# Six turns of the modulation sums by transposes, and the dt projection over column quarters

## What is computed

```python
ada = silu(c) @ w_ada + b_ada          # 9 sequences x 6 sets of 1024
sh_m, sc_m, gt_m, sh_f, sc_f, gt_f = split(ada, 6)
h = rmsnorm(x, g_mix) * (1 + sc_m) + sh_m
u, v, z, xbc, dt_raw = split(h @ w_in)  # dt_raw: 8 columns, one per head
dt = softplus(dt_raw + dt_bias)
...                                     # gMLP heads, convolution and SSD heads
x = x + gt_m * mix
h = rmsnorm(x, g_ffn) * (1 + sc_f) + sh_f
x = x + gt_f * moe(h)                   # top 4 of 32 experts, each 3 matrices of 1024 x 1024
```

## Time and profile before

| | |
|---|---|
| median of 3 runs | 1198.17 us (1196.61 to 1198.84) |
| span of the profiled execution | 1193.2 us |
| what lies around the span, against the median | 5.0 us |
| PE, DVE, ACT, POOL busy in it | 1144.8, 293.9, 153.4, 32.1 us |
| mean granted TensorE clock | 0.985 of full speed |

### The profile page before, as it was taken

How to read it: one execution, slowest core, us unless ns; L and a number is a source line. 1 busy time by engine, 2 the same in 40 slices (tenths; PEclk the granted TensorE clock), 3 DMA queues, 4 the chain that set the end, 5 groups by cost and what they waited for, 6 DMA issues and landing times.

```text
span 1193.2 us, 15523 instructions
## 1 busy us (share of the span) xinstructions
PE 1144.8 (96%) x6471; PEld 532.9 (45%) x6472; DVE 293.9 (25%) x667; ACT 153.4 (13%) x258; POOL 32.1 (3%) x46
## 2 busy tenths in 40 slices
PE   5999999999999999999999999999999999999995
PEld 2666556554353524243535353434343444434332
DVE  3254422422121213030303031212121212121143
ACT  1442141311000000000101010101010101011002
POOL 1030201000000000000000000000000000000000
PEclk9899999999999999999999999999999999999998
DMA  9574567649999999999999999999999999999992
GB/s 381 226 272 156 221 272 313 263 183 429 417 428 422 428 422 427 426 427 427 425 428 428 427 426 429 429 430 426 429 429 430 427 428 429 430 427 420 429 419 90
DMA packets 38788, 452.67 MB, mean 379 GB/s; under 512 B 4176, under 2 KB 6608, under 8 KB 7632
## 3 DMA queue, kind: packets, MB, share of 16 engines
q1 hardware_dynamic: 37984, 449.31, 89.8%
q0 software_dynamic: 752, 2.60, 0.6%
HBM read 447.99 MB, written 3.91 MB: 379 GB/s over the span
## 4 chain that ended last, share of the span: by engine, by line
PE 76%; DMA 19%; ACT 2%; DVE 1%; issue 1%; SPq 0%; DVEq 0%
PE ps L620 75%; DMA arena<-in_w_exp 18%; ACT arena L1320 1%; DMA arena<-in_w_front 1%; DVE arena L1404 1%; DMA arena<-in_xT 1%; PE ps L1007 0%; SPq L517 0%; PE ps L776 0%; DVE arena L1810 0%; DVE arena L1808 0%; DVE arena L1789 0%; ACT arena L1180 0%; PE ps L797 0%; PE ps L1065 0%
## 5 line engine op out<-in xcount | busy, mean ns | idle before, releaser
L620 PE MATMUL ps<-arena 128*64 128x512 f32 (+10 forms) x6226 | 1115.5, 519 | 37.5 <-DMA arena<-in_w_exp 14.3
L620 PEld LDWEIGHTS ps<-arena 128*64 128x64 f32 (+4 forms) x6226 | 505.4, 147 | 638.4 <-issue 568.4
L1320 ACT ACTIVATE arena<-ps 128x1024 f32<-128x1024 f32 x45 | 44.4, 1021 | 516.4 <-PE ps L620 516.4
L1746 DVE TENSOR_SCALAR arena<-ps 128x1024 f32<-128x1024 f32 x15 | 18.3, 1223 | 266.0 <-PE ps L620 266.0
L1404 DVE TENSOR_TENSOR arena<-arena 128x1024 f32<-128x1024 f32 (+11 forms) x91 | 66.2, 749 | 53.1 <-ACT arena L1328 16.8
L1404 DVE TENSOR_TENSOR arena<-arena,ps 128x320 f32<-128x320 f32 (+2 forms) x116 | 57.0, 494 | 69.2 <-PE ps L620 64.2
L1754 DVE TENSOR_SCALAR arena<-ps 128x1024 f32<-128x1024 f32 x15 | 18.4, 1224 | 183.6 <-PE ps L620 183.6
L1328 ACT ACTIVATE arena<-arena 128x1024 f32<-128x1024 f32 x16 | 16.9, 1057 | 243.8 <-DVE arena L1746 228.3
L1739 DVE COPY arena<-arena 128x64 f32 (+3 forms) x32 | 5.0, 193 | 124.9 <-PE ps L620 124.9
L1404 DVE TENSOR_TENSOR arena<-ps,arena 128x64 f32<-128x64 f32 (+10 forms) x39 | 13.2, 354 | 40.1 <-PE ps L620 35.3
L1732 DVE TENSOR_SCALAR arena<-arena 128x64 f32<-128x64 f32 (+3 forms) x96 | 23.0, 302 | 0.1
(11 more groups left out here) (147 smaller groups left out, 176.2 us busy)
## 6 DMA issues: line engine op xcount, KB each, us to landing
arena<-in_w_exp SPq DMA_DIRECT2D x180, 2048.0 KB, 22.0
arena<-in_w_front SPq DMA_DIRECT2D x38, 1024.0 KB, 9.3
arena<-in_w_exp SPq DMA_DIRECT2D x24, 1024.0 KB, 24.0
arena<-in_s0T SPq DMA_DIRECT2D x1, 2048.0 KB, 15.9
out_ssmsT<-arena POOLq DMA_DIRECT2D x4, 512.0 KB, 5.3
arena<-in_xT SPq DMA_DIRECT2D x1, 1280.0 KB, 6.1
out_yT<-arena SPq DMA_DIRECT2D x4, 320.0 KB, 3.3
arena<-in_vec SPq DMA_DIRECT2D x1, 898.0 KB, 18.7
```

What stands on the lines that cost most here:

```text
L620: return pe.matmul(o, l, r, start=start, stop=stop, skip_group_check=True)
L1320: A(moe[name].rearrange("p (a b) -> p a b", a=2), ps[:, bank:bank + 2, :], ACT.Copy).then_inc(done, 1)
L1746: V.tensor_scalar(halves("g"), blocks(0), LIMIT, None, ALU.min).then_inc(g_ready, 1)
```

## The change

Each `ada_turn` becomes four transposes of 128 x 128, one for each chunk of the bank's 512 columns. The two `kk` sums come out apart, and DVE adds them: two additions of bias for the two halves (reading `kk` 0), a wait for its own step, and two additions of `kk` 1. `gather9` leaves the constants, and `ident` moves into their first load, which grows from 73 KB to 128 KB; the second load shrinks.

The dt projection has `w_dt` stationary, 32 columns wide (8 of k, the rest are neighbours that nobody reads), and all 320 columns of `hT` move. The eight products go to four quarters of PSUM bank 3, k and k + 4 adding up in one. ACT copies the bank to a new view `dtT`; behind `ada_sums(GT_M)` PE waits for that copy and runs three matmuls with `gather32`, which add the quarters and turn the result.

A wait of DVE on the ranks uses the ordinary step counter in place of a semaphore of its own.

```diff
             def ada_turn(n, s, bank):
                 pe.wait_ge(adat_ready, n + 1)
-                for m in range(KC):
-                    c = (m % 4) * P
-                    last = mm(ps[:, bank, m * 9:m * 9 + 9], adat[:, n % 2, c:c + P],
-                              cn("gather9")[:, (m // 4) * 9:(m // 4) * 9 + 9])
+                for c in range(0, AW, P):
+                    last = pe.transpose(ps[:, bank, c:c + P], adat[:, n % 2, c:c + P], cn("ident"))
                 last.then_inc(ada_tr, 1)
...
             pe.wait_ge(xbc_line, 1)
-            for t, (t0, n) in enumerate(TILES):
-                for k in range(KC):
-                    last = mm(ps[0:n, 3, t * H:(t + 1) * H], hT[:, k, t0:t0 + n], w_dt[:, k, :], k == 0, k == KC - 1)
-                    if t == 0 and k == 0:
-                        last.then_inc(front_used, 1)
-            last.then_inc(dt_mm, 1)
+            for k in range(KC):
+                g = 32 * (k % 4)
+                last = mm(ps[g:g + 32, 3, 0:T], w_dt[:, k * H:k * H + 32], hT[:, k, :], k < 4, k >= 4)
+                if k == 0:
+                    last.then_inc(front_used, 1)
+            last.then_inc(dtT_mm, 1)
             pe.wait_ge(xbc_line, 5)
             ada_sums(GT_M, 7)
             pe.wait_ge(ld_vec2, 16)
             pe.wait_ge(ld_con, 16)
+            pe.wait_ge(dtT_ready, 1)
+            for t, (t0, n) in enumerate(TILES):
+                last = mm(ps[0:n, 3, 320 + t * H:320 + (t + 1) * H], dtT[:, t0:t0 + n], cn("gather32")[:, 0:H])
+            last.then_inc(dt_mm, 1)
             pe.wait_ge(xbc_line, KC)
... ACT, ahead of the last conv_out
+            act.wait_ge(dtT_mm, 1)
+            A(dtT, ps[:, 3, 0:T], ACT.Copy).then_inc(dtT_ready, 1)
             conv_out(KC - 1)
... DVE, ada_rows
-                tt(ada[:, s], ps[:, bank, 0:KC * 9].rearrange("p (m b) -> p m b", m=KC), wide(bada[:, s, :], 2, 9),
-                   ALU.add).then_inc(ada_ready, 1)
+                turned_sums = ps[:, bank, :].rearrange("p (c k h b) -> p k h c b", c=4, k=2, h=2)[:, :, :, :, 0:9]
+                for h in range(2):
+                    part = ada[:, s, 4 * h:4 * h + 4]
+                    ins = tt(part, turned_sums[:, 0, h], wide(bada[:, s, 4 * h:4 * h + 4], 2, 9), ALU.add)
+                step(ins)
+                for h in range(2):
+                    part = ada[:, s, 4 * h:4 * h + 4]
+                    ins = tt(part, part, turned_sums[:, 1, h], ALU.add)
+                ins.then_inc(ada_ready, 1)
```

More of the change, by code:

```diff
@@ L117 @@
 ROW, ROWW = layout([("g_v", AW), ("dt_bias", H), ("a_log", H), ("d_skip", H), ("b_router", NE)])
-CON, CONW = layout([("ones", P), ("gather9", 2 * (1 + NSEQ)), ("upto", P), ("after", P), ("ident", P), ("before", P),
+CON, CONW = layout([("ones", P), ("ident", P), ("upto", P), ("after", P), ("before", P),
                     ("upto_s", TS), ("after_s", TS), ("seq", NSEQ), ("rep", TS), ("iota", WIDE), ("thr", PASSES), ("eidx", P),
@@ L159, in constants @@
     which = np.arange(P)
-    for half in range(2):
-        for s in range(1 + NSEQ):
-            out[(which % 32 == s) & (which // 32 % 2 == half), CON["gather9"][0] + half * (1 + NSEQ) + s] = 1.0
     put("gather32", (which[:, None] % NE == np.arange(NE)[None, :]).astype(np.float32))
@@ L272, in build @@
         vsq = cat[:, :, 0:AW]
+        dtT = view(acc_at + 2 * H * P, [T])
         def tiny(shape):
@@ L407, in build @@
         w_router = vc("w_router", KC)
-        w_dt = vc("w_dt", KC)
+        w_dt = vec[:, VEC["w_dt"][0]:VEC["w_dt"][0] + (KC - 1) * H + 32]
         w_sp = vc("w_sp", AH)
@@ L435, in build @@
             sem(n) for n in ("line_ready", "xbc_mm", "xbc_line", "conv_begun", "conv_done", "xbc_ready"))
+        dtT_mm, dtT_ready = sem("dtT_mm"), sem("dtT_ready")
         dt_mm, dt_abs, dt_exp, dt_one, dt_ln, dta_ready = (
@@ L1468, in _ @@
             dve.wait_ge(ld_row, 16)
-            step(tt(dtx[:, 0:2, :], ps[:, 3, 0:2 * H].rearrange("p (t h) -> p t h", t=2), wide(rw("dt_bias"), 1, 2), ALU.add))
-            step(tt(dtx[0:TS, 2, :], ps[0:TS, 3, 2 * H:3 * H], rw("dt_bias", TS), ALU.add))
+            step(tt(dtx[:, 0:2, :], ps[:, 3, 320:320 + 2 * H].rearrange("p (t h) -> p t h", t=2), wide(rw("dt_bias"), 1, 2), ALU.add))
+            step(tt(dtx[0:TS, 2, :], ps[0:TS, 3, 320 + 2 * H:320 + 3 * H], rw("dt_bias", TS), ALU.add))
             step(V.tensor_scalar(dtr, dtx, 0.0, None, ALU.max))
@@ L1701, in _ @@
                                              picked[0:rows, a:b, :], ALU.add, ALU.mult)
-            ins.then_inc(rank_read, 1)
-            dve.wait_ge(rank_read, 1)
+            step(ins)
             step(V.tensor_scalar(rank[:, 0:NE, 0:2], rank[:, 0:NE, 0:2], -1.0, None, ALU.add))
```

4 lines of the change are left out of this document (2 added, 2 removed).

## The result

The changed kernel takes 1187.6 us in the median of 5 runs (1185.97 to 1192.68), the kernel before, on the same chip, 1198.28 us (1196.61 to 1199.32): ratio 0.9932, 95% interval 0.9915 to 0.9948. I had predicted 1194.1 us and a range down to 1191.3, so the direction was right and the gain, 10.7 us by these medians, 2.6 times the 4.1 that I had forecast. A part of that is luck. A single run of the changed kernel has a standard deviation of 2.6 us, so the mean of 11 is good to about 0.8 us (an estimate from that scatter).

What follows compares the result with a forecast made beforehand. Bound: PE finishing its first expert unit, then a stream of fixed length. Terms -0.7 - 0.15 - 3.75 + 0.5 = -4.1 against span 1193.2 give 1189.1, plus 5.0 around it 1194.1 us; range 1191.3 to 1197.0.

Steps and rivals of the forecast that it cites:

- the 5.0 around it: Time outside the profiled span: 5.0 us added to put the sum on the median of the runs.
- The clock, the term that failed: v's first tile: PE, sparse from 73.3 to 82.9, probably meets a low clock; +0.5 us, between 0 and 1.7.
- Turn 1 (-0.7): Ahead of the xbc projection: -1.25 on PE, +0.4 on DVE, constants landing 0.14 later; together -0.7 us.
- dt and turn 2 (-0.15): Up to v's first tile: 4.1 us saved, 1.4 left at v's start, -0.15 after waiting for v's second unit.
- turn 1's shift: Turn 1's gain of 0.7 us, applied throughout to later times, which were given on the clock of before.
- the three waits that I named: Ahead of v: PE waits for ada2's last unit (about 2 us), ACT (about 2 us), and `rep_read` until 82.9.
- Turns 3, 4, 5 (-1.25 each): Turns with PE work on both sides and no transfer due: -1.25 us each, -3.75 together.
- my outer bound of -4.1: Largest gain allowed for turns 3 to 5 together, with four transposes at 0.107 us each.
- the first rival: More arrives: v's second unit does not hold PE, the whole 1.4 comes, 1192.7 us, in the extreme 1190.1; chance 0.13.
- a rival with two more low stretches: The clock falls more often in turns and sparse stretches: one more gives 1195.8 us, two 1197.5; chance 0.16.
- The stream of fixed length: After PE finishes its first expert unit, the rest takes a fixed time, so front microseconds gained count at the end.

Runs made afterwards that it cites:

- e1: The kernel before, measured again with no edit: 1197.11 us, ratio 0.9999.
- e6: The kernel before with two dense matmuls of 256 columns added ahead of turn 5, which stays as gathering matmuls: 1195.8 us, ratio 0.9982.
- e10: The kernel before with turn 5 alone done by four transposes and DVE's four additions: 1196.31 us, ratio 0.999.
- e12: The kernel before with the 2 MB of state issued behind v's second unit, not ahead of it: 1196.5 us, ratio 0.9991.
- e13: The kernel before with turn 5's eight gathering matmuls moving 64 columns each in place of 9: 1196.31 us, ratio 0.9988.
- e14: The kernel before with turn 5 by transposes, each of the four done four times: 1196.11 us, ratio 0.9987.
- e3: The kernel before with only the new dt projection, turns still by gathering matmuls: 1197.38 us, ratio 1.0002.
- e11: The kernel before with the new dt projection, and the 2 MB of state issued behind v's second unit: 1197.84 us, ratio 0.9987.
- e2: The kernel before with all six turns by transposes, dt as before: 1192.13 us, ratio 0.9954.
- e4: The changed kernel, measured again with no edit: 1191.57 us, ratio 0.9947 against the kernel before.
- e8: The changed kernel with 28 unneeded transposes of 128 x 128 as filling in PE's waits around turn 1: 1189.52 us, ratio 0.9922.
- e5: The changed kernel with the 2 MB of state issued behind v's second unit, not ahead of it: 1190.0 us, ratio 0.9933.
- e7: The changed kernel with seven unneeded matmuls of 256 columns in PE's waits around turn 1: 1187.87 us, ratio 0.9912.
- e9: The changed kernel with the state issued late, seven filler matmuls around turn 1 and two ahead of turn 5: 1186.4 us, ratio 0.9904.

## Why the prediction was wrong

**The baseline, 3 us.** I put the profiled span of before and "the 5.0 around it" on the median. What lies around the span is 2.0 us. The other 3 were that the profiled execution was quicker than the median, mainly in the clock: its B is 44.2, while the six other kernels with the old dt and the old turn 2 (e1, e6, e10, e12, e13, e14) have 45.9 to 47.4. A sum made against its rows then counts the low stretches of a lucky execution. This is no further term beside the next one: it is why the rows around v had so little to save.

**The clock, the term that failed: +0.5 predicted.** Behind turn 5 the six profiles with gathers of 9 columns (before, e1, e3, e6, e11, e12) each have a low stretch, and E is 46.3 to 46.4. None of the eight with four transposes has it, nor have e13 and e14. The term was -1.6 there, shown by e13 and e14 at the old length of the turn. So the step that failed is the clock's sign: I let the change cost clock around v and nothing elsewhere, and it gave clock back behind turn 5. I had looked for the clock only where the change made PE sparse, and had not read the windows behind the turns for stretches that it could take away. Around v, where I had placed the +0.5, B is 43.9 and 45.9 in the two profiles of the changed kernel against 46.7 in the mean of the seven with the old front: about -1.8 in place of my -0.15 and +0.5. That is less firm than turn 5: the profile of the changed kernel against that of before alone gives -0.3, B scatters by 3 us within the seven, and no experiment separates the clock in it from the rest. Turns 1 to 4 have no such effect that repeats: C and D are the same to 0.01 us within each form.

**Turn 1 (-0.7).** The xbc projection started at 32.09 in place of 32.51, so -0.4 in the two first profiles; in the others the start moves between 31.8 and 34.0 with the low clock that lies over it, and A of the changed kernel (65.7, 65.9) is 0.6 to 0.8 under the shown before and 1.15 under the mean of the seven kernels with the old front (67.0). Right within about its bounds, -0.3 to -1.1. DVE's four additions took 0.61 where I had 0.65.

**dt and turn 2 (-0.15).** The mechanism was right in each step in the changed kernel's profile: v began at 81.94 (82.9 by my sum less turn 1's shift, 82.2), behind the three waits that I named, and PE then waited for v's second unit, which landed at 86.60, 0.85 earlier than before, where I had turn 1's 0.7. That dt gives nothing by itself was measured (e3, e11). But there the reason is not the landing: in e3 PE never waits for the unit, and in e11 the unit is there early; in both profiles the saving goes to the low clock in v's first tile. The landing holds PE where turn 2 is done by transposes (e2, the changed kernel, e4, e8). Whether the whole kernel keeps what e5 gave back is open.

**Turns 3, 4, 5 (-1.25 each).** 1.35, 1.40 and, by e14 less the four-transpose kernels without a wait, 44.7 - 43.4 = 1.3. Mis-sized by about a tenth of a microsecond each: a turn at full clock takes 0.44 and not the 0.48 that I took, and before, turns 4 and 5 took 1.80 and 1.81, where I used turn 3's 1.71 for all. Together they gave 4.05; my outer bound of -4.1 did not follow from its own terms, which give 3 x (1.71 - 0.43) = 3.8. In the first rival, too, 1194.1 less the 1.25 that it adds is 1192.85 and not 1192.7.

**Transposes and the clock.** The Trainium skill, "TensorE: Matmul & The Clock Gate", Part 4 (PE-mode transpose), says that transposes do not count as activity in the way that matmuls do, and by it I had made a rival with two more low stretches. For the float32 transposes here the measurement decides against it: sixteen transposes in place of sixteen narrow records removed a low stretch (e14), and with 28 transposes the clock was at 1.00 where it otherwise fell (e8).

**The sum again.** The two profiles of the changed kernel against the seven with the old front (E against 46.3): A -1.15, B -1.8, C -1.35, D -1.4, E -2.6, G +0.7 (934.7 to 935.4), together -7.6; F goes by chance. The pooled runs give -7.3. Of E's -2.6, -1.3 is the turn, -1.6 the clock, and +0.3 the wait of e4. My 1194.1 lies 4.0 above the pooled 1190.1. Of this, 0.8 is the median of three runs on which I put the sum, against the mean of 91. The other 3.2 are 1.6 behind turn 5, 2.1 around v, 0.45 at turn 1 and 0.3 of the turns, less the 0.7 of G and the 0.3 of that wait, together 3.45 for the 3.2 to be explained.

**The stream of fixed length.** Behind the seam I had put a stream that always takes the same time. It does not. G is 936.3 to 937.9 in e2, e4, e5, e7, e8, e9 and e10, which have 6.8 us of low clock between 348 and 368 us, and 933.7 to 935.3 in the other nine, which have 3.4 us or none there. The loss can be placed: counted from the end of F, SP issues its 29th expert unit at 96.6 us in all sixteen profiles, and the 33rd at 115.1 or 115.2 us without a low stretch there, at 116.8 with 3.4 us of it and at 118.5 with 6.8 us. So PE's clock still sets the time at that place. By the last unit the first two groups are level (880.3 to 881.8), and the third is at 882.4 to 884.3. Six of the seven kernels with all turns by transposes are in the third group, and so is e10, but the first profile of the changed kernel is not. Whether the change brings this loss about or chance does stays open; no experiment tried it.

## What to carry to other kernels

Before a sum is made against one profile, compare that execution's own time, not its span, with the median; where they differ, look for the stretches of low clock that it has or lacks, and price an edit by stages with the same number of them. Where matmuls move few columns behind full weight loads, look at the granted clock behind them as well as at their own time: here the narrow ones cost 1.35 us more than transposes in themselves and 1.6 us in the clock. Saved time at the seam of two dense stretches is worth only what the next transfer and the clock leave of it.

## What the runs showed that I had not expected

- Sixteen records of 9 columns (1.95 us), of 64 columns (2.00) and sixteen transposes of 128 columns (1.97) take the same time, but only the first is followed by 3.4 us of low clock (six profiles of six, against one profile each of the other two).
- Two dense matmuls ahead of the narrow ones did not prevent that stretch (e6, at 180.1 us).
- Moving 2 MB behind a unit of 1 MB in the queue let the unit land at 79.2 in place of 86.6 us.
- Executions of one kernel differ by steps of 1.3 to 1.7 us, each one low stretch of the clock in a stage, and one such place lies in the stream of experts, where the transfers run at 420 to 426 GB/s (345 to 365 us).
